# Experts in 512-column chunks, the last transposes inside a down product, and low weight halves written over the raw units

## The reference, cut to what matters

```python
def swiglu(x, w_gate, w_up, w_down):
    return (jax.nn.silu(x @ w_gate) * (x @ w_up)) @ w_down
# x: tokens x 1024; w_gate, w_up: 1024 x 2816; w_down: 2816 x 1024; 8 experts
for layer in range(DEPTH):                       # DEPTH = 2
    h = h + hybrid_mixer(rms_norm(h), w_in[layer], ...)   # 1024 x 6152 in, 1024 x 1024 out
    hn = rms_norm(h)
    h = h + (swiglu(hn, ...) if layer % 2 == 0 else moe_swiglu(hn, router, ...))
```

## Time and profile before

| what | us |
|---|---|
| median of 3 runs (1725.4 to 1725.92) | 1725.57 |
| profiled execution, first to last instruction (span) | 1724.4 |
| first mixer, and dense layer up to 425 | 425 |
| end of the dense layer and second mixer, 425 to 862 | 437 |
| eight experts, 862 to 1712 | 850 |
| TensorE busy | 1567.3 (91%) |
| VectorE busy | 1212.7 (70%) |
| ScalarE busy | 856.2 (50%) |

### The profile page before, as it was taken

How to read it: one execution, slowest core, us unless ns; L and a number is a source line. 1 busy time by engine, 2 the same in 40 slices (tenths; PEclk the granted TensorE clock), 3 DMA queues, 4 the chain that set the end, 5 groups by cost and what they waited for, 6 DMA issues and landing times.

```text
span 1724.4 us, 25996 instructions
## 1 busy us (share of the span) xinstructions
PE 1567.3 (91%) x10143; PEld 1430.6 (83%) x10143; DVE 1212.7 (70%) x1226; ACT 856.2 (50%) x752; POOL 65.1 (4%) x43
## 2 busy tenths in 40 slices
PE   5989898699996889898599999999999999999995
PEld 5878777699986778777599898998989989899894
DVE  4874634555545874544578888888888888888885
ACT  3423232343423323242267676675767767677672
POOL 0111000000001112000000000000000000000000
PEclk8989999799997989999599999999999999999998
DMA  6323153855402323241979899998999989899880
GB/s 213 128 92 123 49 196 118 297 191 178 145 1 93 127 78 128 78 156 49 343 261 350 292 362 329 308 359 270 361 308 331 361 279 358 300 341 362 283 281 26
DMA packets 267333, 383.98 MB, mean 223 GB/s; under 512 B 9344, under 2 KB 212480, under 8 KB 267136
## 3 DMA queue, kind: packets, MB, share of 16 engines
q1 hardware_dynamic: 267120, 382.50, 65.9%
q10 hardware_dynamic: 144, 0.52, 0.1%
HBM read 381.95 MB, written 1.05 MB: 222 GB/s over the span
## 4 chain that ended last, share of the span: by engine, by line
PE 82%; DVE 8%; issue 4%; ACT 3%; DMA 1%; POOL 1%; SPq 0%; DVEq 0%; ACTq 0%; POOLq 0%
PE ps L469 24%; PE ps L470 24%; PE ps L471 23%; ACT w_hi L1035 2%; PE ps L608 1%; PE ps L625 1%; DVE m_lo L1252 1%; PE ps L621 1%; PE ps L812 1%; PE ps L800 1%; DVE w_lo L1526 1%; PE ps L799 1%; DVE qkvT L1307 1%; PE ps L506 1%; ACT m_hi L928 1%
## 5 line engine op out<-in xcount | busy, mean ns | idle before, releaser
L1526 DVE TENSOR_TENSOR w_lo<-ring,w_hi 128x2048 fp32r<-128x2048 f32 x297 | 680.1, 2290 | 133.6 <-ACT w_hi L1035 133.4
L1035 ACT ACTIVATE w_hi<-ring 128x2048 fp32r<-128x2048 f32 x297 | 569.1, 1917 | 169.5 <-PE ps L471 149.1
L469 PE MATMUL ps<-w_hi,xg_hi 128*128 128x256 f32 x1408 | 406.4, 289 | 7.0 <-ACT gselT L1074 5.0
L470 PE MATMUL ps<-w_lo,xg_hi 128*128 128x256 f32 x1408 | 399.0, 283 | 0.0
L471 PE MATMUL ps<-w_hi,xg_lo 128*128 128x256 f32 x1408 | 398.7, 283 | 0.0
L469 PEld LDWEIGHTS ps<-w_hi,xg_hi 128*128 128x128 f32 x1408 | 270.2, 192 | 13.8 <-issue 10.3
L470 PEld LDWEIGHTS ps<-w_lo,xg_hi 128*128 128x128 f32 x1408 | 270.6, 192 | 3.0
L471 PEld LDWEIGHTS ps<-w_hi,xg_lo 128*128 128x128 f32 x1408 | 270.6, 192 | 0.0
L1252 DVE TENSOR_TENSOR m_lo<-ring,m_hi 128x2048 fp32r<-128x2048 f32 x64 | 145.8, 2289 | 162.5 <-ACT m_hi L928 162.2
L928 ACT ACTIVATE m_hi<-ring 128x2048 fp32r<-128x2048 f32 x64 | 121.7, 1911 | 135.9 <-PE ps L471 127.6
L469 PE MATMUL ps<-w_hi,actT_hi 128*128 128x512 f32 x352 | 140.0, 398 | 17.8 <-DVE actT_lo L1577 17.8
(11 more groups left out here) (270 smaller groups left out, 2270.8 us busy)
## 6 DMA issues: line engine op xcount, KB each, us to landing
ring<-in_moe_w_gate_dram SPq DMA_DIRECT2D x88, 1024.0 KB, 5.7
ring<-in_moe_w_up_dram SPq DMA_DIRECT2D x88, 1024.0 KB, 6.1
ring<-in_moe_w_down_dram SPq DMA_DIRECT2D x88, 1024.0 KB, 5.3
ring<-in_w_in_dram SPq DMA_DIRECT2D x48, 1024.0 KB, 5.2
ring<-in_dense_w_gate_dram SPq DMA_DIRECT2D x11, 1024.0 KB, 5.4
ring<-in_dense_w_up_dram SPq DMA_DIRECT2D x11, 1024.0 KB, 6.4
ring<-in_dense_w_down_dram SPq DMA_DIRECT2D x11, 1024.0 KB, 5.0
ring<-in_w_branch_dram SPq DMA_DIRECT2D x8, 1024.0 KB, 4.9
```

The lines of the kernel that those rows point to most:

```text
L469: mm(dst, xh, yh, start=start, stop=False)
L470: mm(dst, xh, yl, start=False, stop=False)
L1035: go(split_of(j)[0], ring[:, j % SLOTS, :], ACT.Copy).then_inc(hi_ready, 1)
L1526: tt(wl, ring[:, j % SLOTS, :], wh.bitcast(f32), ALU.subtract).then_inc(lo_ready, 1)
```

## The change

1. **Expert chunks.** Gate and up are taken in five chunks of 512 columns and one of 256. A 512-column chunk is two gate units (each four of the eight row blocks), two up units, and two down units. Per expert the 33 units stay.
2. **Last transposes.** Those of the last chunk stand between the two down units of the chunk before (parts 0 and 1), on TensorE, ScalarE and VectorE.
3. **Low halves over the raw units.** VectorE writes the low half into the same slot of `ring`. `w_lo` and `m_lo` go. A slot is free for the next load only when TensorE has used its unit. VectorE's own wait for `unit_used` goes.
4. **Mixers.** Five slots of `ring` instead of three, four buffers `m_hi` instead of three.
5. **`gselT`.** The wait for it moves from the start of a pass to its first up unit.

```diff
-MIX_SLOTS = 3
+MIX_SLOTS = 5
+MIX_HIGH = 4
+EW = 512
+ECHUNK = [EW] * (DFF // EW) + [DFF % EW]
...
-        w_lo = phase("w_lo", f32r, SPLITS, UNIT)
...
+        def expert_order():
+            o = []
+            for c in range(NEC):
+                parts = range(ECHUNK[c] // FF_CHUNK)
+                o += [("gate", c, n) for n in parts] + [("up", c, n) for n in parts]
+                if c:
+                    o += [("down", c - 1, n) for n in range(ECHUNK[c - 1] // FF_CHUNK)]
+            return o + [("down", NEC - 1, n) for n in range(ECHUNK[-1] // FF_CHUNK)]
...
         def split_of(j):
-            return w_hi[:, j % SPLITS, :], w_lo[:, j % SPLITS, :]
+            return w_hi[:, j % SPLITS, :], ring_lo[:, j % SLOTS, :]
...
                 if before is not None:
-                    sp.wait_ge(lo_ready, before + 1)
+                    sp.wait_ge(unit_used, before + 1)
...
-                        sp.wait_ge(lo_ready, e * PASS_UNITS + (i - SLOTS + 1))
+                        sp.wait_ge(unit_used, e * PASS_UNITS + (i - SLOTS + 1))
...
-                pe.wait_ge(gt_ready, q + 1)
-                for j, (kind, c) in enumerate(pass_order()):
-                    if kind == "down" and c == NCHUNK - 1:
-                        transpose_act(q, c)
+                for j, (kind, c, part) in enumerate(expert_order()):
...
+                        if (kind, c, part) == ("up", 0, 0):
+                            pe.wait_ge(gt_ready, q + 1)
+                        nk = KD // parts_of(c)
...
+                        for k in range(nk):
+                            kk = part * nk + k
+                            last = product(ps[n][:, 0:ECHUNK[c]], xg_hi[:, kk, :], xg_lo[:, kk, :],
+                                           vh[:, k, :], vl[:, k, :], kk == 0, kk == KD - 1)
...
+                    if (kind, c, part) == ("down", NEC - 2, 0):
+                        transpose_act(q, NEC - 1)
...
-                        if i >= SPLITS:
-                            act.wait_ge(unit_used, i - SPLITS + 1)
+                        if n_split[0] >= MIX_HIGH:
+                            act.wait_ge(unit_used, i - MIX_HIGH + 1)
...
             def split_low(off, j):
                 dve.wait_ge(hi_ready, off + (j + 1))
-                dve.wait_ge(unit_used, off + (j - SPLITS + 1))
```

More of the change, by code:

```diff
@@ L347, in mixer_split @@
         def mixer_split(n, k):
-            return tuple(m[:, n % SPLITS, :].rearrange("p (k n) -> p k n", k=k) for m in (m_hi, m_lo))
+            return tuple(m.rearrange("p (k n) -> p k n", k=k)
+                         for m in (m_hi[:, n % MIX_HIGH, :], ring_lo[:, n % MIX_SLOTS, :]))
         def w_in_units(layer, col):
@@ L830, in expert_pass @@
                         for jj in range(2):
+                            jt = 2 * part + jj
                             for f in range(2):
                                 col = slice(f * 512, (f + 1) * 512)
-                                last = product(ps[4 + f][:, :], actT_hi[:, c % 2, jj, :], actT_lo[:, c % 2, jj, :],
+                                last = product(ps[4 + f][:, :], actT_hi[:, c % 2, jt, :], actT_lo[:, c % 2, jt, :],
                                                vh[:, jj, col], vl[:, jj, col],
-                                               c == 0 and jj == 0, c == NCHUNK - 1 and jj == 1)
+                                               c == 0 and jt == 0, c == NEC - 1 and jt == ECHUNK[c] // P - 1)
@@ L836, in expert_pass @@
                     else:
                         n = 2 * (c % 2) + (kind == "up")
-                        if kind == "gate":
-                            pe.wait_ge(ffn_act, q * NCHUNK + NCHUNK + c - 1)
+                        if kind == "gate" and part == 0:
+                            pe.wait_ge(ffn_act, q * NEC + NCHUNK + c - 1)
                             if c == 1:
                                 pe.wait_ge(moe_drained, q * 2 + 1)
-                        vh, vl = (v.rearrange("p (k n) -> p k n", k=KD) for v in (wh, wl))
@@ L846, in expert_pass @@
                     last.then_inc(unit_used, 1)
-                    if kind == "gate" and c:
+                    if kind == "gate" and c and part == parts_of(c) - 1:
                         transpose_act(q, c - 1)
+                    if (kind, c, part) == ("down", NEC - 2, 0):
+                        transpose_act(q, NEC - 1)
                 if not final:
@@ L923, in split_upto @@
                         act.wait_ge(loaded[slot], value)
-                        if i >= SPLITS:
-                            act.wait_ge(unit_used, i - SPLITS + 1)
-                        if n_split[0] < SPLITS and base:
+                        if n_split[0] >= MIX_HIGH:
+                            act.wait_ge(unit_used, i - MIX_HIGH + 1)
+                        elif base:
                             act.wait_ge(unit_used, base)
-                        go(m_hi[:, n_split[0] % SPLITS, :], ring[:, slot, :], ACT.Copy).then_inc(hi_ready, 1)
+                        go(m_hi[:, n_split[0] % MIX_HIGH, :], ring[:, slot, :], ACT.Copy).then_inc(hi_ready, 1)
                         n_split[0] += 1
@@ L1078, in expert_pass @@
                 off = q * PASS_UNITS + STATIC_UNITS
-                for j, (kind, c) in enumerate(pass_order()):
-                    if kind == "gate":
+                for j, (kind, c, part) in enumerate(expert_order()):
+                    if kind == "gate" and part == parts_of(c) - 1:
                         act.wait_ge(unit_used, off + j + 1)
-                        act.wait_ge(ffn_a1, q * NCHUNK + NCHUNK + c - 1)
-                        go(th_f[:, c % 2, 0:FF_CHUNK], ps[2 * (c % 2)][:, 0:FF_CHUNK], ACT.Tanh,
+                        act.wait_ge(ffn_a1, q * NEC + NCHUNK + c - 1)
+                        go(th_f[:, c % 2, 0:ECHUNK[c]], ps[2 * (c % 2)][:, 0:ECHUNK[c]], ACT.Tanh,
                            scale=0.5).then_inc(ffn_th, 1)
@@ L1246, in split_upto @@
                         dve.wait_ge(hi_ready, i + 1)
-                        if i >= SPLITS:
-                            dve.wait_ge(unit_used, i - SPLITS + 1)
-                        if n_split[0] < SPLITS and base:
-                            dve.wait_ge(unit_used, base)
-                        b = n_split[0] % SPLITS
-                        tt(m_lo[:, b, :], ring[:, plan[i][0], :], m_hi[:, b, :].bitcast(f32),
+                        slot = plan[i][0]
+                        tt(ring_lo[:, slot, :], ring[:, slot, :], m_hi[:, n_split[0] % MIX_HIGH, :].bitcast(f32),
                            ALU.subtract).then_inc(lo_ready, 1)
@@ L1584, in expert_pass @@
                 V.tensor_copy(gcur.unsqueeze(2), quad(gw, NT)[:, :, bass.ds(e, 1)]).then_inc(gcur_ready, 1)
[L1585 removed]
+                for j, (kind, c, part) in enumerate(expert_order()):
                     b = c % 2
[L1587 to L1589 removed]
+                    ending = part == parts_of(c) - 1
+                    if kind == "gate" and ending:
+                        dve.wait_ge(ffn_th, q * NEC + NCHUNK + c + 1)
+                        stt(a1[:, b, 0:ECHUNK[c]], th_f[:, b, 0:ECHUNK[c]], 1.0, ps[2 * b][:, 0:ECHUNK[c]],
                             ALU.add, ALU.mult).then_inc(ffn_a1, 1)
```

96 lines of the change are left out of this document (53 added, 43 removed).

## The result

The changed kernel takes 1679.34 us against 1725.74 for the one before on the same chip: ratio 0.9732, 95% interval 0.9719 to 0.9745. That is 46 us less, where 35.3 were forecast, and 3.7 us under the range. The profiled execution has a span of 1676.4 us, 48.0 less than before.

A forecast was written before the change was run, and what follows sets the result against it. TensorE alone was taken to set the pace inside a pass. Terms 10.7 + 17.8 + 5.2 + 1.6 = 35.3 us off the 1724.4 us span gave 1689.1, plus 1.2 around it: 1690 us, range 1683 to 1706.

The forecast's parts named there:

- Low halves in place: Dense layer and experts: writing the low half over its own input costs nothing extra, and later loads cause no wait.
- Wide matmuls: Experts' gate and up units: 12 matmuls of 512 columns replace 24 of 256, saving 0.067 us a unit, 10.7 us.
- The Trainium skill's formula: Rival on matmul spacing, N/2.4 + 2.5 ns: the wide pairs save only 4.8 us, total 1696 us; chance 0.02.
- The last transposes: End of each expert pass: a down unit issued between covers TensorE's wait for `actT_lo`, so all 17.8 us go.
- Uncovered: Rival at the last down unit: 1.5 of the 2.4 us wait remain each pass, 12 us, total 1702; chance 0.10.
- The wait for `gselT`: Start of an expert pass: moving the wait gains 0.75 us a pass, 5.2 us over 7 passes; bounds 0 and 7.
- The loop's branch: TensorE's queue at a pass start: hidden under the 1.0 us gap before, it costs at most all of it.
- Mixers: Convolution groups in two mixer layers: four `m_hi` save 0.8 us a layer, 1.6 us; bounds 0 and 5.6.
- Wide steps break the split chain: Rival in wide expert chunks: 1 us more per chunk makes a 0.5 us wait, 20 us, total 1710; chance 0.10.
- the slack: Wide expert chunk: the low half is ready at t + 5.5, needed at t + 6.03, so 0.5 us to spare.
- Loads slower: Rival in the experts' loads: at 3.3 us a unit passes take 109 us, 26 us slower, total 1751; chance 0.03.
- More is gained: Rival: mixers give their whole 5.6 us and the pass starts their whole 7, 5.8 more, total 1684; chance 0.07.

The follow-up runs named there:

- The run with late transposes: The changed kernel with the last transposes put back directly ahead of the last down unit: 1696.0 us, ratio 0.9828.
- the other layout: The changed kernel with all operands at multiples of 64 bytes and TensorE's stationary operands directly behind the ring: 1671.9 us, ratio 0.9684.

## Why the prediction missed

46 us came, and 35.3 were summed. The step that failed is the term that the prediction put at nothing, "Low halves in place"; it comes first.

*Low halves in place, "nothing": the step that failed.* The prediction asked what writing over one's own input costs VectorE, and not what reading from another place does to TensorE. The other place gives 0.7 us a pass (gate and up 0.55, down 0.2), 5.8 in the experts, and 2.5 in the dense layer: 8.3 us, most of the 11 by which the sum of 35.3 was short.

*Wide matmuls, 10.7 us: about right.* The line's own numbers, 24 x 0.1196 - 12 x 0.2333, give 0.071 a unit and 11.3 us, not 0.067 and 10.7. Measured is 9.9 us for the spacing, with the price of two groups of transposes for one of four (0.42) nearly met: 0.35 and 0.09. The row of the wide shape carried over (233.6 became 232.2), while the narrow one had already come down from 119.6 to 118.3 by the low halves' place. The Trainium skill's formula ("TensorE: Matmul & The Clock Gate", section "Back-to-back issue gap") would have given 4.8 us, further off than the rows: the trace does not agree with it here. The section gives that formula for a single matmul and states about 131 ns at 512 columns for a stream of them; no unit here is under 228 ns.

*The last transposes, 17.8 us: the mechanism right, the size too small.* The prediction took the idle time in the list, 2.40. From the transposes' start to the down unit's it is 2.78, now 0.14: 2.65 a pass and 1.27 in the last, 19.8 us. The run with late transposes gave 16 to 17 only since the wide chunks have the shorter wait of 1.9. On top comes one stretch at the lower clock in the profiled execution before, 1.4 us, of which the prediction says nothing. "Uncovered" and its 12 us didn't come, but narrowly: 0.06 us were left of the 0.2 in the sum.

*The wait for `gselT`, 5.2 us: right.* 1.0 gained less 0.16 to 0.2 given back, 5.6 in the run with the wait put back. The loop's branch cost nothing that shows.

*Mixers, 1.6 us: wrong, nothing that can be told.* In the first mixer the two waits of the earlier trace rows became one:

```profile
57.34 0.39 PE L501 MATMUL ps<-mx_hi,m_hi 128*128 128x256 f32 x1 [1.90 <-DVE ring_lo L1286]
```

The microsecond gained was gone before the dense layer, which starts at 326.4 instead of 326.0. Mixer 1's 2.4 us less in the two profiled executions can't be told from scatter: with three `m_hi` it lasted 346.1 us, with four 344.8 to 346.8.

*Rivals.* "Wide steps break the split chain" didn't happen, and the slack is 0.7, not 0.5. "Loads slower" didn't: DMA holds 354 GB/s at a share of 1.00 mid-pass and nothing waits for it. "More is gained" was the right side, for a reason that it didn't name.

Sum by what was measured: wide 9.9, low halves' place 8.3, transposes 19.8, `gselT` 5.6, a stretch of the lower clock 1.4, which is 45.0; the spans differ by 48.0, mixer 1's 2.4 is most of the rest, and 0.6 stay open.

## To carry over

A wait of TensorE that is two microseconds long can cost more than its length: count the matmuls behind it that run at the lower clock, pass by pass. Price a wait by the distance of the starts around it, not by the idle time in the list (2.65 against 2.40 here). Where a kernel is bound by TensorE, measure the distance of matmul starts per operand placement, since moving a buffer is an edit to the time; here one layout gave 8 us of 1680 for no work. And when a buffer is written in place, ask how long its slot stays taken: three slots instead of five cost 97 us.

## What the runs showed of the hardware

- The same matmuls stand closer or wider by the SBUF addresses of their operands alone. In the kernel before, 256 columns took 119.8 ns and 117.6 in the dense layer with `w_lo` 32 bytes further up, and 512 columns 233.6 ns and 231.6 with everything from `w_hi` on 32 bytes further up. In the changed kernel 512 columns took 232.2 ns and 229.1 with the other layout. For 512, 229 came where the weights' halves, the ring and the still operand start at the same residue modulo 64 and the still operand lies between 106624 and 131200, with low halves in the ring; with `w_lo` behind `w_hi` and the rest equal it was 231.6. For 256 the rule is open: 32 bytes between the halves gave 2 ns, 32 bytes at the other operand in the new layout took 1.0.
- The granted clock fell to 0.50 behind waits of 1.9 to 2.5 us without matmuls, in 1 to 5 of 8 passes, and was back after five to eight matmuls of 512 columns, 1.3 to 1.6 us dearer together. Which pass it hits changes from kernel to kernel.
- The first matmul behind a group of transposes has 0.08 to 0.09 us more to its next one than the others (0.20 instead of 0.12 at 256 columns, 0.32 instead of 0.23 at 512), in every group looked at in the passes of both kernels.
